# Modulation vectors summed over the partitions: plain fp32 sums as the moving operand, one row each, in place of split halves as the stationary operand

## The chip, the cores and the metric

The kernel runs on one core of one Trainium2 chip. The metric is the time of one execution on the device, in microseconds (us); the median of several runs counts.

## What is computed

The reference is a two-part transformer: two layers with Fourier, neighbourhood and latent attention branches and a feed-forward part, on 512 latent and 256 context tokens of width 1024, and then a second block with a mixture of experts. Every normalization is followed by a modulation, whose shift, scale and gate vectors come from a conditioning vector. Only this matters here:

```python
silu_c = jax.nn.silu(c)
silu_cc = jax.nn.silu(c_ctx)
for l in range(DEPTH):
    ...
    sh1, sc1, g1, sh2, sc2, g2 = [m[:, None, :] for m in jnp.split(silu_c @ w_mod[l] + b_mod[l], 6, axis=-1)]
    csh1, csc1, cg1, csh2, csc2, cg2 = jnp.split(silu_cc @ w_mod[l] + b_mod[l], 6, axis=-1)
    a_lat = x_lat * (1 + sc1) + sh1
```

Each `w_mod` is 1024 x 6144 in fp32; the second block has its own, with one conditioning vector.

## The kernel before

Activations lie transposed in SBUF: features on the 128 partitions, tokens along the row. A dense layer (`run_dense`) goes through *pieces*: a piece is one output tile of 128 features. For each piece SP loads 128 columns of weights (`w_raw`, two buffers in turn), ACT copies them to fp32r (`w_hi`, L1118), DVE subtracts that from the original (`w_lo`, L1128), and TensorE (PE) multiplies: `w_hi` and `w_lo` with the high half of the activations (L1101, L1102), `w_hi` with their low half (L1104). Thus three fp32r products stand for one fp32 product. Results lie in PSUM banks 0 to 3 for even pieces and 4 to 7 for odd ones; ACT or DVE takes them out. SP waits for `w_lo` of the piece two before (`lo_ready`) and then loads the next weights.

The modulation vectors of what comes later are made beside such a dense layer, by `Vectors` (L815), a *background* of `run_dense`. It takes `w_mod` in chunks of 512 columns. A chunk is four loads of 256 x 512 values (`vec_w`, two buffers, L857). For each of the `nv` conditioning vectors DVE multiplies the weights by the vector's value of each partition and adds up over the eight row tiles (`vec_acc`, L877 and L880). What is left is a sum over the partitions, for which TensorE serves: `vec_acc` is split into an fp32r half on ACT (`vec_hi`, L902) and the rest on DVE (`vec_lo`, L865), and these are the *stationary* operands, 128x128 at a time, against two columns of ones (`ones_r`). So the vector comes out with features on the partitions, 128 of them a matmul, in bank 3:

```python
pe.wait_ge(*self.sem(vec_lo, k + 1))
for q in range(4):
    for v in range(self.nv):
        o = 3 * BANK + ((4 * k + q) * self.nv + v) * 2
        for part in (self.hi, self.lo):
            m = pe.matmul(ps[:, o:o + 2], part[:, v, q * P:(q + 1) * P], ones_r[:], start=(part is self.hi), stop=(part is self.lo))
```

After the last chunk DVE adds the bias (L889) and 1 to the scales (L894).

The order on each engine is written out by hand, by the number of the piece. At piece n an engine first does its part of the splitting for piece n+1, then `behind(n)`, the background's share, and then takes out the results of piece n; TensorE does `behind(n)` ahead of its matmuls of piece n. If the last sums of a chunk fall at piece n, its halves are made at n+1 (ACT behind the cast of the weights, DVE behind `w_lo`), and its matmuls stand ahead of piece n+2. `vec_used` counts the steps of sums that DVE has done; SP waits for it before it loads the next `vec_w`, and what SP issues behind that, the weights of the next piece included, comes later. What is left when the pieces have run out is done by `rest` at the stage's end.

`Vectors` runs three times: in the first projection of layer 0 (20 pieces, 8 chunks, two vectors, a chunk every 2 pieces from piece 4 on, thus the last chunk's matmuls are in `rest`), in the feed-forward stage of layer 0 (60 pieces, 12 chunks, two vectors, a chunk every 4 pieces from piece 2 on) and in that of layer 1 (60 pieces, 12 chunks, one vector). During the first of these POOL makes bias tables for the neighbourhood attention: it gathers small pieces from DRAM (L1753, eight DMAs a table, three tables) and adds masks (L1756).

## Time and profile before

| | |
|---|---|
| median of 3 runs | 3252.98 us (3251.86 to 3255.18) |
| the profiled execution's own time | 3246.34 us |
| its span in the profile | 3244.5 us |
| PE busy | 2950.4 us (91%) |
| DVE busy | 1679.8 us (52%) |
| ACT busy | 1228.2 us (38%) |
| POOL busy | 411.5 us (13%) |
| mean granted clock of TensorE | 0.956 |
| PE, small matmuls of the vectors (L912) | 208 of `vec_hi`, 208 of `vec_lo` |
| DVE, sums (L880) | 364 of 128x512, 257.7 us |

The profile comes from one execution, whose instructions are recorded; its time is not that of the other runs. The span is what the records cover. PEld is the loading of stationary operands, which runs beside matmuls. The ends of matmuls are modelled, so the time that a matmul takes from the ones behind it is read from the distance of the starts. The clock of TensorE is given as a share of full speed (1.00 is 2.4 GHz, 0.50 is 1.2 GHz). Register, branch, semaphore and DMA-issuing instructions don't count as busy.

### The profile page before, as it was taken

What the parts mean: (1) busy time and instruction counts of PE and PEld (TensorE: products, weight loads), DVE (VectorE), ACT (ScalarE), POOL (GpSimd) and SP (SyncE); (2) the same over time, 40 slices, a digit from 0 to 9 for tenths busy, and PEclk for the clock granted to TensorE, in tenths of its full rate; (3) what the DMA queues carried; (4) which work ended last, traced back from release to release, by engine and by line L of the source; (5) the groups of instructions that cost most, each with busy time, mean ns of one, the idle gap of its engine ahead of it and who ended that gap; (6) DMA issues with size and microseconds to landing.
All of it is one profiled execution on the core that took longest, in us unless ns stands there. A gap on an engine that the chain in (4) does not pass through costs nothing. (4 is left out here: it accounts for less than half of the span.)

```text
span 3244.5 us, 37650 instructions
## 1 busy us (share of the span) xinstructions
PE 2950.4 (91%) x15073; PEld 2353.4 (73%) x15073; DVE 1679.8 (52%) x2334; ACT 1228.2 (38%) x1821; POOL 411.5 (13%) x395
## 2 busy tenths in 40 slices
PE   7898889999979999999798799998999968876995
PEld 4787556888868888887587457886888736554784
DVE  3575665223345555543416554446655354645896
ACT  5324545122243211221535443225322144535884
POOL 4400400000010000002402100000000004202332
PEclk9899999999989999999899899999999988897997
DMA  7861101222114443332610104324656236334962
GB/s 205 147 176 37 24 1 39 63 65 60 55 39 130 120 121 104 117 90 49 95 53 16 24 10 107 98 72 143 186 160 181 72 47 72 150 109 144 374 238 78
DMA packets 397873, 330.15 MB, mean 102 GB/s; under 512 B 38038, under 2 KB 340484, under 8 KB 397572
## 3 DMA queue, kind: packets, MB, share of 16 engines
q1 hardware_dynamic: 384196, 304.56, 33.3%
q0 software_dynamic: 13248, 23.13, 3.5%
q8 instruction: 120, 1.97, 0.3%
q14 instruction: 53, 0.43, 0.1%
q10 hardware_dynamic: 256, 0.07, 0.0%
HBM read 331.96 MB, written 30.33 MB: 112 GB/s over the span
## 5 line engine op out<-in xcount | busy, mean ns | idle before, releaser
L1101 PE MATMUL ps<-ahi,w_hi 128*128 128x512 f32 (+1 forms) x2264 | 770.8, 354 | 6.6 <-DVE w_lo L1128 6.6
L1102 PE MATMUL ps<-ahi,w_lo 128*128 128x512 f32 (+1 forms) x2264 | 768.0, 353 | 0.0
L1128 DVE TENSOR_TENSOR w_lo<-w_raw,w_hi 128x1024 fp32r<-128x1024 f32 (+2 forms) x244 | 352.0, 1444 | 389.9 <-ACT w_hi L1118 388.1
L1101 PEld LDWEIGHTS ps<-ahi,w_hi 128*128 128x128 f32 x2264 | 428.1, 189 | 69.3 <-DVE w_lo L1128 9.8
L1104 PE MATMUL ps<-alo,w_hi 128*128 128x512 f32 (+1 forms) x2264 | 474.1, 352 | 0.0
L1102 PEld LDWEIGHTS ps<-ahi,w_lo 128*128 128x128 f32 x2264 | 428.4, 189 | 59.6
L1118 ACT CAST w_hi<-w_raw 128x1024 fp32r<-128x1024 f32 (+2 forms) x244 | 285.3, 1171 | 488.7 <-PE ps L1104 378.8
L1104 PEld LDWEIGHTS ps<-alo,w_hi 128*128 128x128 f32 x2264 | 376.8, 189 | 58.8
L880 DVE SCALAR_TENSOR_TENSOR vec_acc<-vec_w,csilu,vec_acc 128x512 f32<-128x512 f32 x364 | 257.7, 753 | 10.8 <-DMA vec_w<-in_w_mod 5.7
L1204 POOL TENSOR_TENSOR xsum<-x 128x768 f32<-128x768 f32 (+1 forms) x4 | 7.2, 1801 | 1421.8 <-DVE x L1189 1421.8
L1189 DVE SCALAR_TENSOR_TENSOR x<-ps,mod,x 128x512 f32<-128x512 f32 x80 | 51.4, 668 | 250.6 <-PE ps L1104 235.2
L1101 PE MATMUL ps<-hhi,w_hi 128*128 128x512 f32 (+1 forms) x462 | 157.8, 356 | 0.0
L1102 PE MATMUL ps<-hhi,w_lo 128*128 128x512 f32 (+1 forms) x462 | 157.5, 355 | 0.0
L1224 ACT CAST hhi<-hf 128x768 fp32r<-128x768 f32 (+1 forms) x44 | 32.0, 728 | 282.1 <-DVE hf L1232 282.1
L3105 ACT CAST e_hi<-e_raw 128x2048 fp32r<-128x2048 f32 x69 | 131.6, 1913 | 14.9 <-DMA e_raw<-in_w_up 9.6
L1670 POOL TENSOR_SCALAR prob<-prob,nm 128x512 f32<-128x512 f32 (+3 forms) x64 | 79.5, 1242 | 394.5 <-DVE nm L1595 394.5
L1306 DVE TENSOR_TENSOR gp<-sg,ps 128x768 f32<-128x768 f32 (+1 forms) x32 | 26.3, 821 | 196.7 <-PE ps L1104 179.6
L1297 ACT ACTIVATE sg<-ps 128x768 f32<-128x768 f32 (+1 forms) x48 | 33.8, 705 | 241.0 <-PE ps L1104 241.0
L1164 ACT COPY proj<-ps 128x512 f32<-128x512 f32 (+2 forms) x58 | 39.6, 748 | 191.9 <-PE ps L1104 180.0
L1971 PE MATMUL ps<-mla_pt,proj 128*128 128x512 f32 x192 | 102.5, 616 | 0.0
L1102 PEld LDWEIGHTS ps<-hhi,w_lo 128*128 128x128 f32 x462 | 86.9, 188 | 13.0
L1101 PEld LDWEIGHTS ps<-hhi,w_hi 128*128 128x128 f32 x462 | 86.9, 188 | 13.0
(525 smaller groups left out, 5299.4 us busy)
## 6 DMA issues: line engine op xcount, KB each, us to landing
vec_w<-in_w_mod SPq DMA_DIRECT2D x128, 512.0 KB, 3.9
w_raw<-in_w_in SPq DMA_DIRECT2D x102, 512.0 KB, 4.3
e_raw<-in_w_gate SPq DMA_DIRECT2D x46, 512.0 KB
e_raw<-in_w_up SPq DMA_DIRECT2D x46, 512.0 KB
e_raw<-in_w_down SPq DMA_DIRECT2D x46, 512.0 KB
w_raw<-in_w_ffn_gate SPq DMA_DIRECT2D x44, 512.0 KB, 3.9
w_raw<-in_w_ffn_up SPq DMA_DIRECT2D x44, 512.0 KB, 3.9
w_raw<-in_w_ffn_down SPq DMA_DIRECT2D x32, 704.0 KB, 4.7
```

Of the source, the lines that this page charges most:

```text
L880: m = dve.scalar_tensor_tensor(out=acc, in0=w, scalar=f, in1=acc, op0=ALU.mult, op1=ALU.add)
L1101: pe.matmul(o, whi[:, j, b0 + b, :], hi[:, b, t0:t0 + tn], start=(b == 0), stop=False)
L1102: pe.matmul(o, wlo[:, j, b0 + b, :], hi[:, b, t0:t0 + tn], start=False, stop=False)
L1104: m = pe.matmul(o, whi[:, j, b0 + b, :], lo[:, b, t0:t0 + tn], start=False, stop=(b == nb - 1))
L1118: act.copy(whi[:, j, 0:d.blocks, :], raw_of(d, i, jj)).then_inc(hi_ready[j].sem, 1)
L1128: dve.tensor_tensor(wlo[:, j, 0:d.blocks, :], raw_of(d, i, jj), whi[:, j, 0:d.blocks, :].bitcast(F32), ALU.subtract).then_inc(lo_ready[j]. ...
L1164: m = act.copy(o_, s_) if scale is None else act.activation(o_, s_, ACT.Identity, scale=scale)
L1189: m = dve.scalar_tensor_tensor(out=xo, in0=ps[:, b + t0:b + t0 + tn], scalar=mod[:, v, bass.ds(i * 2 + (gate + jj), 1)], in1=xo, op0=ALU.m ...
L1297: act.activation(sg[:, jj, :], ps[:, 4 * BANK * jj:4 * BANK * jj + T], ACT.Sigmoid).then_inc(gated.sem, 1)
L1670: pool.tensor_scalar(self.prob[:, j, slot, 0:u.keys], self.prob[:, j, slot, 0:u.keys], self.nm[:, j, slot, 3:4], None, ALU.mult).then_inc( ...
L1971: m = pe.matmul(ps[:, bank:bank + LAT], weight(b, j), self.pt[:, s % 3, :], start=(b == 0), stop=(b == kt - 1))
L3105: act.copy(whi[:, n % HI, :], raw[:, n % RAW, :]).then_inc(e_hi.sem, 1)
```

## The change

The sums are no longer split. They become the *moving* operand of a plain fp32 matmul, 512 columns at once, one matmul a vector. The stationary operand is a window of `pick_row`, a table of 128 x 47 zeros with one column of ones in the middle: the window of `rows` columns (`rows` = chunks x vectors: 16, 24 and 12) that has the ones at place r puts the sum over the partitions into row r of the output and adds zeros to all other rows. All chunks accumulate in one region of bank 3 (`start` only for row 0, `stop` only for the last row), which ends as a matrix of `rows` x 512. DVE copies that to SBUF (into a buffer of sums that is free by then), TensorE transposes it in four parts of 128 columns, and DVE adds the bias as before, with another pattern of addresses. `vec_acc` has two buffers, so that DVE goes on with the next chunk at once. ACT has no part any more. TensorE waits for `vec_used`, that is for the sums themselves, at the same piece as before; the copy comes one piece after the last matmuls, the transposes another piece later, and the bias at the end, two pieces later than before.

```diff
@@ -56,6 +56,7 @@
+VEC_ROWS = 24
...
-        vec_used, vec_hi, vec_lo, vec_mm, vec_chain = (tally(n) for n in ("vec_used", "vec_hi", "vec_lo", "vec_mm", "vec_chain"))
+        vec_used, vec_mm, vec_chain = (tally(n) for n in ("vec_used", "vec_mm", "vec_chain"))
...
-        ones_r = sb(root, "ones_r", [P, 2], F32R)
+        pick_row = sb(root, "pick_row", [P, 2 * VEC_ROWS - 1])
...
                     ch.link(dve.memset(ones[:], 1.0))
-                    ch.mark(dve.tensor_copy(ones_r[:], ones[:, 0:2]))
+                    ch.link(dve.tensor_scalar(pick_row[:], ones[:, 0:2 * VEC_ROWS - 1], 0.0, None, ALU.mult))
+                    ch.mark(dve.tensor_copy(pick_row[:, VEC_ROWS - 1:VEC_ROWS], ones[:, 0:1]))
...
                 self.raw = sb(c, "vec_w", [P, 2, self.STEP, self.CN])
-                self.acc = sb(c, "vec_acc", [P, self.nv, self.CN])
-                self.hi = sb(c, "vec_hi", [P, self.nv, self.CN], F32R)
-                self.lo = sb(c, "vec_lo", [P, self.nv, self.CN], F32R)
+                self.acc = sb(c, "vec_acc", [P, 2, self.nv, self.CN])
+                self.rows = self.chunks * self.nv
+                self.row = self.acc[0:self.rows, self.chunks % 2, 0, :]
                 self.norm_first = norm_first
                 self.when = [start + n // self.per_chunk * pieces + n % self.per_chunk * pieces // self.per_chunk for n in range(self.steps)]
                 last = [self.when[(k + 1) * self.per_chunk - 1] for k in range(self.chunks)]
                 self.at = {}
                 for s_, n in enumerate(self.when):
                     self.at.setdefault(n, []).append(s_)
-                self.hi_at = {n + 1: k for k, n in enumerate(last)}
-                self.lo_at = {n + 1: k for k, n in enumerate(last)}
                 self.mm_at = {n + 2: k for k, n in enumerate(last)}
-                assert len(self.hi_at) == self.chunks
-                self.end = last[-1] + 4
-                self.c0 = {t: t.base for t in (*vec_loaded, vec_used, vec_hi, vec_lo, vec_mm, vec_chain)}
+                assert len(self.mm_at) == self.chunks
+                self.copied_at, self.turned_at = last[-1] + 3, last[-1] + 4
+                self.end = last[-1] + 6
+                self.c0 = {t: t.base for t in (*vec_loaded, vec_used, vec_mm, vec_chain)}
...
             def run(self, who, eng, n):
-                {"sp": self.sp, "dve": self.dve, "act": self.act, "pe": self.pe}[who](eng, n)
+                if who != "act":
+                    {"sp": self.sp, "dve": self.dve, "pe": self.pe}[who](eng, n)
...
@@ -857,20 +859,14 @@
                     sp.dma_start(self.raw[:, s_ % 2], self.wv[:, self.STEP * kp:self.STEP * (kp + 1), c0:c0 + self.CN]).then_inc(vec_loaded[s_ % 2].sem, 16)
 
             def dve(self, dve, n):
-                if n in self.lo_at:
-                    k = self.lo_at[n]
-                    dve.wait_ge(*self.sem(vec_hi, k + 1))
-                    if k >= 1:
-                        dve.wait_ge(*self.sem(vec_mm, k))
-                    dve.tensor_tensor(self.lo[:], self.acc[:], self.hi[:].bitcast(F32), ALU.subtract).then_inc(vec_lo.sem, 1)
                 for s_ in self.at.get(n, []):
                     k, kp = s_ // self.per_chunk, s_ % self.per_chunk
                     dve.wait_ge(*self.sem(vec_loaded[s_ % 2], 16 * (s_ // 2 + 1)))
-                    if kp == 0 and k >= 1:
-                        dve.wait_ge(*self.sem(vec_lo, k))
+                    if kp == 0 and k >= 2:
+                        dve.wait_ge(*self.sem(vec_mm, k - 1))
                     for q in range(self.STEP):
                         for v, a in enumerate(self.cols):
-                            acc, w = self.acc[:, v, :], self.raw[:, s_ % 2, q, :]
+                            acc, w = self.acc[:, k % 2, v, :], self.raw[:, s_ % 2, q, :]
                             f = csilu[:, a, self.STEP * kp + q:self.STEP * kp + q + 1]
                             done = (s_ * self.STEP + q) * self.nv + v
                             if kp == 0 and q == 0:
@@ -881,44 +877,45 @@
                             m.then_inc(vec_chain.sem, 1)
                     dve.wait_ge(*self.sem(vec_chain, (s_ + 1) * self.STEP * self.nv))
                     dve.sem_inc(vec_used.sem, 1)
+                if n == self.copied_at:
+                    dve.wait_ge(*self.sem(vec_mm, self.chunks))
+                    dve.tensor_copy(self.row, ps[0:self.rows, 3 * BANK:4 * BANK]).then_inc(vec_chain.sem, 1)
                 if n == self.end - 1:
-                    dve.wait_ge(*self.sem(vec_mm, self.chunks))
+                    dve.wait_ge(*self.sem(vec_mm, self.chunks + 1))
                     t0, nt = self.first // P, self.chunks * 4
                     for v in range(self.nv):
-                        src = ps[:, 3 * BANK:3 * BANK + nt * 2 * self.nv].rearrange("p (t v two) -> p t v two", v=self.nv, two=2)[:, :, v, 0]
-                        m = dve.tensor_tensor(self.dst[:, v, t0:t0 + nt], src, self.bias[:, t0:t0 + nt], ALU.add)
+                        src = ps[:, 3 * BANK:3 * BANK + 4 * self.rows].rearrange("p (q k v) -> p k q v", q=4, v=self.nv)[:, :, :, v]
+                        m = dve.tensor_tensor(self.dst[:, v, t0:t0 + nt].rearrange("p (k q) -> p k q", q=4), src,
+                                              self.bias[:, t0:t0 + nt].rearrange("p (k q) -> p k q", q=4), ALU.add)
                     m.then_inc(vec_chain.sem, 1)
-                    dve.wait_ge(*self.sem(vec_chain, self.steps * self.STEP * self.nv + 1))
+                    dve.wait_ge(*self.sem(vec_chain, self.steps * self.STEP * self.nv + 2))
                     for s_ in (1, 2, 4, 5) if self.nv == 2 else (1, 4):
                         if s_ * KT >= t0:
                             dve.tensor_scalar(self.dst[:, 0:self.nv, s_ * KT:(s_ + 1) * KT], self.dst[:, 0:self.nv, s_ * KT:(s_ + 1) * KT], 1.0, None, ALU.add)
 
-            def act(self, act, n):
-                if n in self.hi_at:
-                    k = self.hi_at[n]
-                    act.wait_ge(*self.sem(vec_used, (k + 1) * self.per_chunk))
-                    if k >= 1:
-                        act.wait_ge(*self.sem(vec_mm, k))
-                    act.copy(self.hi[:], self.acc[:]).then_inc(vec_hi.sem, 1)
-
             def pe(self, pe, n):
                 if n in self.mm_at:
                     k = self.mm_at[n]
-                    pe.wait_ge(*self.sem(vec_lo, k + 1))
+                    pe.wait_ge(*self.sem(vec_used, (k + 1) * self.per_chunk))
+                    for v in range(self.nv):
+                        r = k * self.nv + v
+                        own = pick_row[:, VEC_ROWS - 1 - r:VEC_ROWS - 1 - r + self.rows]
+                        m = pe.matmul(ps[0:self.rows, 3 * BANK:4 * BANK], own, self.acc[:, k % 2, v, :], start=(r == 0),
+                                      stop=(r == self.rows - 1), skip_group_check=True)
+                    m.then_inc(vec_mm.sem, 1)
+                if n == self.turned_at:
+                    pe.wait_ge(*self.sem(vec_chain, self.steps * self.STEP * self.nv + 1))
                     for q in range(4):
-                        for v in range(self.nv):
-                            o = 3 * BANK + ((4 * k + q) * self.nv + v) * 2
-                            for part in (self.hi, self.lo):
-                                m = pe.matmul(ps[:, o:o + 2], part[:, v, q * P:(q + 1) * P], ones_r[:], start=(part is self.hi), stop=(part is self.lo))
+                        o = 3 * BANK + q * self.rows
+                        m = pe.transpose(ps[:, o:o + self.rows], self.row[:, q * P:(q + 1) * P], ident[0:self.rows, 0:self.rows])
                     m.then_inc(vec_mm.sem, 1)
 
             def ended(self):
                 for b in range(2):
                     vec_loaded[b].base += 16 * len([s_ for s_ in range(self.steps) if s_ % 2 == b])
                 vec_used.base += self.steps
-                for t in (vec_hi, vec_lo, vec_mm):
-                    t.base += self.chunks
-                vec_chain.base += self.steps * self.STEP * self.nv + 1
+                vec_mm.base += self.chunks + 1
+                vec_chain.base += self.steps * self.STEP * self.nv + 2
```

How the instructions stand afterwards, at the places of interest. First DVE in the first projection, where the first chunk is complete and the second begins; a row is line, operation, output and inputs by name, shape, and in brackets the semaphores that it waits for. Before:

```order
L880 SCALAR_TENSOR_TENSOR vec_acc<-vec_w,csilu,vec_acc 128x512 [waits vec_chain] x3
L1128 TENSOR_TENSOR w_lo<-w_raw,w_hi 128x1024 [waits vec_chain,hi_ready1]
L865 TENSOR_TENSOR vec_lo<-vec_acc,vec_hi 128x1024 [waits vec_hi]
L877 TENSOR_SCALAR vec_acc<-vec_w,csilu 128x512 [waits vec_lo,vec_loaded0]
L877 TENSOR_SCALAR vec_acc<-vec_w,csilu 128x512
L880 SCALAR_TENSOR_TENSOR vec_acc<-vec_w,csilu,vec_acc 128x512 [waits vec_chain] x2
```

With the change the same place on DVE reads so:

```order
L876 SCALAR_TENSOR_TENSOR vec_acc<-vec_w,csilu,vec_acc 128x512 [waits vec_chain] x3
L1125 TENSOR_TENSOR w_lo<-w_raw,w_hi 128x1024 [waits vec_chain,hi_ready1]
L873 TENSOR_SCALAR vec_acc<-vec_w,csilu 128x512 [waits vec_loaded0]
L873 TENSOR_SCALAR vec_acc<-vec_w,csilu 128x512
L876 SCALAR_TENSOR_TENSOR vec_acc<-vec_w,csilu,vec_acc 128x512 [waits vec_chain] x2
```

The subtraction is gone, and the next chunk's sums wait for their load alone.

Second, DVE at the end of the same stage (`vec_5` is the bias, `mod_8` the vectors), from the last sums to the branch out of the block. Before:

```order
L880 SCALAR_TENSOR_TENSOR vec_acc<-vec_w,csilu,vec_acc 128x512 [waits vec_chain,vec_loaded1]
L880 SCALAR_TENSOR_TENSOR vec_acc<-vec_w,csilu,vec_acc 128x512 [waits vec_chain] x3
L865 TENSOR_TENSOR vec_lo<-vec_acc,vec_hi 128x1024 [waits vec_chain,vec_mm,vec_hi]
L889 TENSOR_TENSOR mod_8<-ps,vec_5 128x32 [waits vec_mm]
L889 TENSOR_TENSOR mod_8<-ps,vec_5 128x32
L894 TENSOR_SCALAR mod_8<-mod_8 128x2x8 [waits vec_chain]
```

With the change, again DVE at the end of the stage:

```order
L876 SCALAR_TENSOR_TENSOR vec_acc<-vec_w,csilu,vec_acc 128x512 [waits vec_chain,vec_loaded1]
L876 SCALAR_TENSOR_TENSOR vec_acc<-vec_w,csilu,vec_acc 128x512 [waits vec_chain] x3
L882 COPY vec_acc<-ps 16x512 [waits vec_chain,vec_mm]
L888 TENSOR_TENSOR mod_8<-ps,vec_5 128x32 [waits vec_mm]
L888 TENSOR_TENSOR mod_8<-ps,vec_5 128x32
L894 TENSOR_SCALAR mod_8<-mod_8 128x2x8 [waits vec_chain]
```

The subtraction has made room for a copy of 16 rows, which waits for TensorE.

Third, TensorE at that end: the last dense matmuls of the stage, what the vectors add, and the next stage's first. With the change:

```order
L1101 MATMUL ps<-alo,w_hi 128x256 x8
L903 MATMUL ps<-vec_acc,pick_row 16x512 [waits vec_used]
L903 MATMUL ps<-vec_acc,pick_row 16x512
L910 MATMUL ps<-ident,vec_acc 128x16 [waits vec_chain]
L910 MATMUL ps<-ident,vec_acc 128x16 x3
L1009 UNCONDITIONAL_BRANCH
```

Where L903 stands there were sixteen matmuls L912, in turn of `vec_hi` and `vec_lo`, the first of which waited for `vec_lo`; L910 is new.

## Rows read from the trace of the kernel before

**Rows 1.** The page: busy us (share of the span) x instructions of TensorE.

```profile
PE 2950.4 (91%) x15073; PEld 2353.4 (73%) x15073; DVE 1679.8 (52%) x2334; ACT 1228.2 (38%) x1821; POOL 411.5 (13%) x395
```

**Rows 2.** Stretches: us, busy us (count) by engine, clock, DMA share, GB/s.

```profile
0.00:60.00 60.00, 43.85 (x211) 22.31 (x211) 19.19 (x50) 24.52 (x46) 28.78 (x60) 1.00 0.70 216
60.00:160.00 100.00, 87.58 (x468) 75.85 (x469) 48.59 (x56) 44.13 (x64) 43.95 (x50) 0.90 0.87 151
1100.00:1300.00 200.00, 200.00 (x1183) 177.13 (x1182) 104.12 (x133) 37.00 (x38) 0.00 (x0) 1.00 0.38 114
```

**Rows 3.** Tiles of sums' halves: count, ns min/median/max, first and last start.

```profile
L912 PE MATMUL ps<-ones_r,vec_hi x208: 165/250/371, 127.3 to 2524.0; 128*128 128x2 f32 x104
L865 DVE TENSOR_TENSOR vec_lo<-vec_acc,vec_hi x32: 682/1217/1767, 122.5 to 2521.6; 128x1024 fp32r<-128x1024 f32 x20, 128x512 fp32r<-128x512 f32 x12
```

**Rows 4.** Timeline, PE, end of a group: start us, us, line, tiles, count.

```profile
127.26 0.17 PE L912 MATMUL ps<-ones_r,vec_hi 128*128 128x2 f32 x1
128.96 0.47 PE L1101 MATMUL ps<-ahi,w_hi 128*128 128x512 f32 x1
129.28 0.39 PE L1102 MATMUL ps<-ahi,w_lo 128*128 128x512 f32 x1
129.51 0.40 PE L1101 MATMUL ps<-ahi,w_hi 128*128 128x512 f32 x1
```

**Rows 5.** Timeline, PE: plain fp32 matmuls (each is two records).

```profile
53.17 3.62 PE L311 MATMUL ps<-proj,mod_c 128*2 128x256 f32 x16
928.76 10.59 PE L606 MATMUL ps<-vec_w,ones 128*128 128x512 f32 x32 [1.93 <-ACT vec_w L622]
```

**Rows 6.** Timeline, DVE, 122 to 164 us; in brackets the idle time before.

```profile
122.50 1.77 DVE L865 TENSOR_TENSOR vec_lo<-vec_acc,vec_hi 128x1024 fp32r<-128x1024 f32 x1
124.37 1.66 DVE L877 TENSOR_SCALAR vec_acc<-vec_w,csilu 128x512 f32<-128x512 f32 x2
140.00 2.74 DVE L880 SCALAR_TENSOR_TENSOR vec_acc<-vec_w,csilu,vec_acc 128x512 f32<-128x512 f32 x4 [4.07 <-DMA vec_w<-in_w_mod]
152.07 1.32 DVE L1128 TENSOR_TENSOR w_lo<-w_raw,w_hi 128x1024 fp32r<-128x1024 f32 x1 [9.32 <-ACT w_hi L1118]
162.17 1.23 DVE L1128 TENSOR_TENSOR w_lo<-w_raw,w_hi 128x1024 fp32r<-128x1024 f32 x1
```

**Rows 7.** SP and POOL issues, landing of the 132.41 issue, ACT's cast behind it.

```profile
132.41 0.64 SPq L1040 DMA_DIRECT2D w_raw<-in_w_in  x1
DMA to landing us min/median/max: 18.6/18.6/18.6
130.37 6.04 POOL L1753 DMA_DIRECT2D proj<-rpb_rows  x8 [0.32 <-POOL na_bias L1756]
150.99 1.04 ACT L1118 CAST w_hi<-w_raw 128x1024 fp32r<-128x1024 f32 x1 [12.51 <-DMA w_raw<-in_w_in]
```

**Rows 8.** PE around the stall: timeline, and two stretches with the clock.

```profile
155.11 0.37 PE L912 MATMUL ps<-ones_r,vec_hi 128*128 128x2 f32 x1 [9.21 <-DVE vec_lo L865]
158.54 0.77 PE L1101 MATMUL ps<-ahi,w_hi 128*128 128x512 f32 x1
149.00:150.00 1.00, 0.00 (x0) 0.84 1.14 262
163.00:164.00 1.00, 1.00 (x5) 0.84 0.82 104
```

**Rows 9.** Timeline, PE and DVE, end of the first stage.

```profile
260.68 1.12 PE L1104 MATMUL ps<-alo,w_hi 128*128 128x256 f32 x8
264.90 0.27 PE L912 MATMUL ps<-ones_r,vec_hi 128*128 128x2 f32 x1 [3.09 <-DVE vec_lo L865]
267.78 0.29 DVE L889 TENSOR_TENSOR mod<-ps,vec 128x32 f32<-128x32 f32 x2 [2.94 <-PE ps L912]
```

**Rows 10.** Timeline, PE: transposes of the prologue; tile view, DVE copies from PSUM.

```profile
25.34 1.09 PE L302 MATMUL ps<-ident,proj 128*128 128x128 f32 x8
L1606 DVE COPY proj<-ps x18: 404/682/692, 331.3 to 2838.0; 128x512 f32<-128x512 f32 x14, 128x256 f32<-128x256 f32 x4
```

## Prediction

> **What bounds the kernel now.** I read the busy times first, then a table of stretches, then the tiles that the change touches, then the timelines of single engines around them. TensorE is busy 2950.4 of 3244.5 us [rows 1]. Background sums for the modulation vectors run beside three dense stages: the first projection (60 to 268 us, 8 chunks of two vectors), the feed-forward of layer 0 (960 to 1530 us, 12 chunks of two vectors) and that of layer 1 (2220 to 2590 us, 12 chunks of one vector). In the feed-forward stages TensorE is busy 200.00 of 200.00 us at clock 1.00, while DVE has 104.12 and ACT 37.00 us [rows 2]: there only TensorE's own work counts, and DVE's and ACT's vector work is hidden. The first projection is different: from 60 to 160 us the clock is 0.90 and TensorE is busy 87.58 of 100 us [rows 2], so it stands still somewhere.
>
> **What is removed.** ACT's cast of each chunk's sums and DVE's subtraction (32 of each; the subtraction 1217 ns at the median) go [rows 3]. Hidden in the feed-forward stages, they are worth nothing there: the cover is the dense matmuls, and without it the two would cost some 2.5 us a chunk. TensorE loses 416 small matmuls, 208 for each half [rows 3].
>
> **TensorE, per chunk.** With two vectors a chunk is 16 small matmuls. The first starts at 127.26, the dense ones go on at 128.96; the first dense interval behind them is 0.32 us where the next is 0.23 us [rows 4]. So a group costs 1.70 + 0.09 = 1.79 us, 0.112 us each, and 0.90 us with one vector. The new group is one plain fp32 matmul of 512 columns per vector. Its price: 16 records of 512 and 16 of 256 columns in 10.59 us, thus 24 units of 512 columns; less a tail of some 0.2 us that is 0.43 us a record, two records a matmul [rows 5]. That gives 0.86 us a vector, 1.72 us for two. That its stationary operand has 12 to 24 columns, not 128, should not matter: records with 2 stationary columns and 256 moving ones take 3.62 us for 16, 0.22 us each, the same rate [rows 5]. The gain is 0.07 us a chunk with two vectors and 0.04 us with one: 18 chunks x 0.07 + 12 x 0.04 = 1.8 us (two of the first stage's chunks are counted below). Added are four transposes a stage. Eight of 128x128 take 1.09 us, 0.12 us each without the tail [rows 10], so 0.5 us in each feed-forward stage, 1.0 us together. Net: **0.8 us gained**. Bounds: nothing to 2 us.
>
> The Trainium skill (FP8 and Floating Point Precision, TensorE Precision Notes) counts four passes for true fp32. Four dense passes of 0.23 us [rows 4] would be 0.92 us a matmul, against the 0.86 us of the row; the sum would then lose 52 x 0.06 = 3 us. I go by the row, which is the very kind of matmul.
>
> The copy out of PSUM (DVE, 682 ns at the median for 128x512 [rows 10]) and the transposes' wait for it cost nothing in the feed-forward stages: DVE runs the copy right behind the splitting for the next piece, TensorE asks for it one piece later, and a piece is 8 us or more. Behind the waiting transposes stands that next piece; it would be late only if the copy were 5 us late. The tables' block of zeros costs two tiny DVE instructions at the start, where DVE waits for loads: nothing. The loads themselves are unchanged in number and order on SP's queue; POOL's is not passed.
>
> **The stall at 146 us.** TensorE waits 9.21 us, until 155.11, for DVE's low half of a chunk's sums [rows 8]. But DVE's low half stood behind its splitting of weights, which started at 152.07 and ended at 153.39 [rows 6], and that behind ACT's cast at 150.99, which had waited 12.51 us for a transfer of weights [rows 7]. This transfer was issued at 132.41 on SP's queue, among eight gathers that POOL issues from 130.37 on, and took 18.6 us [rows 7]. Then TensorE worked through the small group first, at half clock, and real work began at 158.54; the clock was at its lower level from about 149.7 to 163.3 (0.84 is the mean of a microsecond with 0.32 of it at half clock) [rows 8].
>
> Now the sums of that chunk are complete before 146 us (DVE's last adds end at 142.74 [rows 6]), TensorE waits for them alone, and the 1.7 us of new matmuls fall into the stall. It then restarts when the weights are split: 153.4 in place of 155.11, 1.7 us earlier, and without 3.43 us of small matmuls at half clock, which are 1.7 us at full clock. If nothing else moved, that is **3.4 us**.
>
> Something else moves. DVE's subtraction at 122.50 takes 1.77 us before the next chunk's sums start at 124.37 [rows 6]. SP's loads of that chunk wait for these sums, and the weight transfer is issued behind them on the same queue. So I take the issue at 132.41 to come 1.9 us earlier, at 130.5, when one gather is out and not three. I take the landing to move by the same 1.9 us. Total for the stall: **5.3 us**. Lower bound 3.4 (the landing stays, since the gathers stay). Upper bound: TensorE's standstill shrinks to 4 us or less, and the clock may never fall; it fell 3.7 us after TensorE stopped. The 8.2 us at half clock from 155.1 on would then lose nothing, 4 us more: 9.3 us.
>
> The Trainium skill (DMA: Bandwidth & Descriptors, Queues, rings and completion order) says that a DMA engine serves the queues with work in turn, packet by packet. By that the weights still share with the gathers that come later, so the landing would move by no more than the issue does; if the queues were served in order of issue it would move by several us. The single 18.6 us does not tell the two apart.
>
> **The end of the first stage.** The last chunk comes after the last dense piece. TensorE stops at 261.80, ACT casts, DVE subtracts, the small group runs from 264.90 (partly at half clock) and DVE's add starts at 267.78 [rows 9]: 5.98 us. Now: 4 records x 0.43 = 1.72, the drain of the last 0.17, copy 0.68, four transposes 0.36 with 0.27 of tail, two hand-overs of 0.05: 3.3 us. The add and what follows are the same. **2.7 us gained**; bounds 1.5 (some of it at half clock) to 3.
>
> **Sum.** 0.8 + 5.3 + 2.7 = 8.8 us. The profiled execution took 3246.34 us with a span of 3244.5; it would be 3237.5. It lies 6.6 us below the median of the runs, 3252.98, so the unprofiled runs may stall a little longer. I carry the difference over: 3252.98 - 8.8 = **3244.2 us**. About 0.2% (6.5 us) is what a measurement of this kernel can tell from no change.
>
> **Rivals.**
> 1. *The clock stays up in the stall.* If the weights land at 148 us or before, TensorE resumes before the clock falls. Gain 9.3 in place of 5.3, sum 12.8, time 3240.2. For it: the standstill is only about 2 us longer than the time in which the clock fell. Against it: the landing must move by more than the issue.
> 2. *The stall is given back one piece later.* DVE has two steps of sums between one splitting (ended 153.39) and the next (162.17 to 163.40) [rows 6]: 8.3 us without the subtraction, about as long as a piece of TensorE at full clock. These sums need loads that stand in the same crowded queue. If the landings don't move and these sums are late by 3 us or so, the stall yields 0 to 1 us, and the total is 0.8 + 0.5 + 2.7 = 4 us: 3249 us, no measurable change. For it: DVE is in order, and three loads queue behind the gathers.
> 3. *Slower: the new matmuls run at half clock.* The feed-forward stages have no slack on TensorE. If matmuls that use 12 to 24 columns of the array let the clock fall, each of the 52 costs 0.86 us more; all of them are 45 us, 3289 us. It decides from 18 matmuls on (8.8 + 6.5 us over 0.86). Against it: the prologue, with 2 stationary columns in most matmuls, holds 1.00 from 0 to 60 us [rows 2], and the small groups of today don't bring it down either [rows 2].
>
> **How the numbers follow.** Forecast as worked out 0.45 (its own range 3241 to 3246.5), rival 1 0.20, rival 2 0.28, rival 3 0.07. The first two are faster by over 0.2%: 0.65. Same 0.28, slower 0.07. The range takes in rival 1 and most of rival 2: 3237 to 3251.
>
> **What would show it.** In the new profile: two fp32 matmuls a chunk as four records 0.43 us apart, at clock 1.00 in the feed-forward stages; TensorE's wait near 146 us ended by a weight splitting and not by sums, at 151.5; dense work there 5 us or more ahead of before; the last dense matmul of the first stage to DVE's add in 3.3 us; both feed-forward stages within 1 us of before. I am wrong if the weight transfer lands no earlier, if a new wait follows within 20 us, or if records of the new matmuls are longer than 0.43 us apart.

## The result and the profile after

The changed kernel takes **3230.6 us** (median of 6 runs, 3227.54 to 3235.27); the kernel before, in runs beside them, 3251.0 us (3241.18 to 3255.18). The ratio is 0.9941, 95% interval 0.9925 to 0.9957. The same two kernels, compared again on two later occasions, gave 0.9960 (0.9946 to 0.9973) and 0.9945 (0.9929 to 0.9960): 13 to 18 us. The prediction was 3244.2 us, range 3237 to 3251: right in its sign, but the gain is about twice the 8.8 us of its sum, and the time lies below the range.

The profiled execution took 3230.32 us with a span of 3228.5 us. The stretches that answer to [rows 2] and [rows 8] (microseconds; then each engine's busy time, TensorE's granted clock, DMA share, GB/s):

```profile
60.00:160.00 100.00, 94.77 (x494) 78.95 (x495) 56.16 (x64) 43.76 (x64) 46.06 (x50) 0.95 0.75 169
149.00:150.00 1.00, 1.00 (x3) 0.10 (x1) 1.00 (x3) 0.79 (x2) 0.00 (x0) 1.00 0.84 295
1100.00:1300.00 200.00, 200.00 (x1125) 169.01 (x1124) 98.62 (x128) 31.93 (x34) 0.00 (x0) 1.00 0.38 113
```

From 60 to 160 us TensorE is busy 94.77 us, 7.2 more than in [rows 2], and the clock is 0.95 there. What is left of half clock lies between 60 and 90 us, where both kernels have some (0.83, 0.90 and 0.76 in the three tens of microseconds before, 0.83, 0.92 and 0.74 after): the prediction read the 0.90 of [rows 2] as the stall's alone. In the feed-forward stage it is busy throughout, as before, at clock 1.00: rival 3 (new matmuls at half clock) is out. The timeline of TensorE between 136 and 151 us, against [rows 8]:

```profile
136.99 1.12 PE L1101 MATMUL ps<-alo,w_hi 128*128 128x256 f32 x8
139.79 0.50 PE L1098 MATMUL ps<-ahi,w_hi 128*128 128x512 f32 x1 [1.68 <-DVE w_lo L1125]
...
148.37 1.89 PE L903 MATMUL ps<-vec_acc,pick_row 128*16 128x512 f32 x4
150.19 0.50 PE L1098 MATMUL ps<-ahi,w_hi 128*128 128x512 f32 x1
```

The wait of 9.21 us is gone, and with it the half clock behind it: rival 1's picture, but by more than rival 1 had it, since the only wait left there is 1.68 us at 139.79. It belongs to another piece: the transfer that is crowded now was issued at 122.27 and took 12.8 us to land. The transfers that the prediction reasoned about have moved far. This is POOL's timeline, for [rows 7]:

```profile
92.42 5.30 POOL L1750 DMA_DIRECT2D proj<-rpb_rows  x7 [0.30 <-POOL na_bias L1753]
104.77 0.77 POOL L1750 DMA_DIRECT2D proj<-rpb_rows  x1 [7.04 <-issue]
117.93 6.05 POOL L1750 DMA_DIRECT2D proj<-rpb_rows  x8 [0.32 <-POOL na_bias L1753]
```

POOL's third table of gathers goes at 117.93 us, not at 130.37 [rows 7]. In the kernel before, the eighth gather of the second table waited longer as well:

```profile
94.63 5.31 POOL L1753 DMA_DIRECT2D proj<-rpb_rows  x7 [0.30 <-POOL na_bias L1756]
113.10 0.76 POOL L1753 DMA_DIRECT2D proj<-rpb_rows  x1 [13.16 <-issue]
```

At 113 us nothing that the prediction speaks of has happened yet: the first subtraction whose absence could free DVE is the one at 122.50 [rows 6]. So something in the change acts earlier and elsewhere. This was the question of the experiments.

The end of the first stage, for [rows 9], is TensorE's timeline and then DVE's:

```profile
251.15 1.12 PE L1101 MATMUL ps<-alo,w_hi 128*128 128x256 f32 x8
252.19 1.89 PE L903 MATMUL ps<-vec_acc,pick_row 128*16 128x512 f32 x4
254.86 0.41 PE L910 MATMUL ps<-ident,vec_acc 16*128 16x16 f32 x4 [0.77 <-DVE vec_acc L882]
```

```profile
254.12 0.68 DVE L882 COPY vec_acc<-ps 16x512 f32<-16x512 f32 x1 [6.02 <-PE ps L903]
255.31 0.29 DVE L888 TENSOR_TENSOR mod<-ps,vec 128x32 f32<-128x32 f32 x2 [0.51 <-PE ps L910]
```

From the end of the dense matmuls (252.27) to DVE's add (255.31) are 3.04 us, where they were 5.98 and the prediction said 3.3.

### The profile page after: what moved, and what is told of

Same layout as the page of the kernel before. It is cut to its first block and busy times, and to the rows that moved or that the text cites. A ratio compares the mean times of both kernels' runs of the same rounds, so it can differ in the third digit from the quotient of the medians.

```text
span 3228.5 us, 36929 instructions
## 1 busy us (share of the span) xinstructions
PE 2949.7 (91%) x14773; PEld 2309.6 (72%) x14773; DVE 1651.2 (51%) x2306; ACT 1203.4 (37%) x1789; POOL 417.6 (13%) x395
## 3 DMA queue, kind: packets, MB, share of 16 engines
q0 software_dynamic: 13248, 23.13, 3.0%
## 5 line engine op out<-in xcount | busy, mean ns | idle before, releaser
L876 DVE SCALAR_TENSOR_TENSOR vec_acc<-vec_w,csilu,vec_acc 128x512 f32<-128x512 f32 x364 | 261.5, 764 | 13.6 <-DMA vec_w<-in_w_mod 9.1
L1294 ACT ACTIVATE sg<-ps 128x768 f32<-128x768 f32 (+1 forms) x48 | 33.8, 705 | 241.0 <-PE ps L1101 241.0
L1218 ACT ACTIVATE sg<-ps 128x768 f32<-128x768 f32 (+1 forms) x44 | 31.0, 704 | 179.1 <-PE ps L1101 178.8
```

Source lines behind the costliest of these rows:

```text
L876: m = dve.scalar_tensor_tensor(out=acc, in0=w, scalar=f, in1=acc, op0=ALU.mult, op1=ALU.add)
L1294: act.activation(sg[:, jj, :], ps[:, 4 * BANK * jj:4 * BANK * jj + T], ACT.Sigmoid).then_inc(gated.sem, 1)
```

## The experiments

There were sixteen runs: thirteen kernels with one edit or two, and three repetitions of the kernels before and after. Times are medians; every ratio is to the kernel before in runs on the same chip, comes from all runs of both, and can differ from the quotient of the medians by up to 0.0011. Two lengths recur: that of the **first stage**, from TensorE's first `ahi,w_hi` matmul to its first `latent_sq,ones` matmul behind 230 us, read from each profile (208.4 us before, 195.7 after), and the start of POOL's third table.

### Undo one part of the change: the wait, or DVE's work

`before_again` is the kernel before, `after_again` the changed one.

> The kernel before, unchanged, for a second profile. The profile of before stalled TensorE for 9.2 us at 146 us (13 us with the half clock), that of the change for 1.7 us. Theory A (the change removes the stall): the stall is here again, 9 us or more, and the time is 3245 to 3255 us. Theory B (the gathers' timing is luck and the two profiles differ by it): the stall is here of another size, under 5 us, or absent, and the time differs from the 3251.0 us of before by 5 us or more.

> The change, unchanged, for a second profile and as the base of the two variants. Theory A: a stall of 0 to 3 us near 140 us, time 3227 to 3235 us. Theory B: a stall of 5 us or more also happens with the change.

`after_oldwait` puts the wait back: TensorE's group also waits for a one-column DVE copy at the place of the old subtraction (the edit, shortened).

```diff
+self.late_at = {n + 1: k for k, n in enumerate(last)}
+self.late = sb(c, "vec_late", [P, 1])
 # dve
+if n in self.late_at: dve.tensor_copy(self.late[:], ones[:, 0:1]).then_inc(vec_late.sem, 1)
 # pe
+pe.wait_ge(*self.sem(vec_late, k + 1))
```

> The change, but TensorE's matmuls of a chunk also wait for a mark (a copy of one column on DVE) that stands where DVE's subtraction stood, behind the splitting of the next weights. DVE's time stays free. If the place of the wait makes the gain, the matmuls fall behind the stall again: 3.5 us or more slower than the change (3234 or more). If DVE's earlier sums and the earlier transfers behind them make it: within 2 us of the change.

`after_dvetime` puts DVE's work back (a subtraction of 128 x nv x 512 at the old place), and TensorE does not wait for it.

> The change, plus a subtraction of the old size on DVE at the old place, whose result nobody reads; TensorE doesn't wait for it. If the sums that start 1.8 us earlier, and with them the loads, make the gain at the stall: most of it goes, 8 to 12 us slower than the change (3239 to 3243), with a stall over 6 us at 140 to 155 us in the profile. If the place of the wait makes it: within 2 us of the change.

Measured: before_again 3249.63 us, 1.0003 (0.9990 to 1.0017). after_again 3232.23, 0.9960. The stall is there again in before_again (9.0 us), and after_again has a wait of 3.6 us: the two profiles did not differ by luck. after_dvetime 3231.90, 0.9948 (0.9934 to 0.9962): DVE's work costs nothing that can be measured. after_oldwait 3252.19, 1.0019 (1.0006 to 1.0033): all the gain gone, which looks like proof that the wait was worth 20 us. The profile says no. The first stage of after_oldwait is 198.6 us, as short as in after_again (199.0), and POOL's third table goes at 116.3 us. Its time is lost in the feed-forward stages, where all dense matmuls are the same: the part that the kernel before runs from 924 to 1529 us takes 614.6 us where the changed kernel takes 604.5, and the one from 2191 to 2593 us takes 408.3 in place of 401.9: together 16.5 of the 20 us. One period of the feed-forward in each (stretches, granted clock 1.00 in both):

```profile
1306.90:1341.80 34.90, 34.90 (x197) 29.31 (x196) 18.78 (x24) 7.07 (x8) 0.00 (x0) 1.00 0.41 120
```

```profile
1279.20:1314.90 35.70, 35.70 (x198) 29.68 (x197) 18.84 (x25) 7.06 (x8) 0.00 (x0) 1.00 0.39 119
```

The first is the changed kernel, the second after_oldwait: the same matmuls, never idle, 0.8 us longer. What did differ was where they read from. In the built programs, pick_row (47 columns, 192 bytes) takes the room of ones_r (2 columns, 32 bytes), so the tiles behind it lie 160 bytes further on in their partitions: proj, na_bias, ahi, alo, vec_w and the first stage's w_raw start at 96 modulo 256 bytes before, and at 0 after. And the mark tile of after_oldwait, 4 bytes that take up 32, pushes the feed-forward's w_raw, w_hi and w_lo from 192 to 224 modulo 256 (they are at 32 in the kernel before).

### Move the tiles, change no instruction

`before_moved` is the kernel before with one tile widened, `after_unmoved` the changed kernel with all tiles back at their old places modulo 256, `oldwait_moved` is after_oldwait with a mark tile of 64 bytes, which puts the feed-forward's three tiles at 0 modulo 256, `after_all64` aligns x, the mods and the latent attention's tiles too (warm allocated ahead of mods, three pads).

```diff
-ones_r = sb(root, "ones_r", [P, 2], F32R)
+ones_r = sb(root, "ones_r", [P, 2 * 24 - 1], F32R)[:, 0:2]                 # before_moved
-pick_row = sb(root, "pick_row", [P, 2 * VEC_ROWS - 1])
+pick_row = sb(root, "pick_row", [P, 72])[:, 0:2 * VEC_ROWS - 1]            # after_unmoved
-self.late = sb(c, "vec_late", [P, 1])
+self.late = sb(c, "vec_late", [P, 16])                                     # oldwait_moved
```

> Kernel before, with one edit: the tile ones_r is 47 columns wide in place of 2 (only its first 2 are used). No instruction changes; every SBUF tile behind it lies 160 bytes further on in its partition, which is where the change puts them (in the built programs ahi, alo, proj, na_bias and the first stage's w_raw, w_hi, w_lo begin at 96 modulo 512 bytes before and at 256 after: from 32 to 0 modulo 64). Theory A (places: the 20 us of the change come from where the tiles lie, by faster DMA landings in the first stage and closer matmuls later): ratio to before 0.994 to 0.996, about 3235 us, POOL's third table of gathers from about 117 us, the stall at 154 us gone or under 4 us. Theory B (waits: they come from the vectors' chain, which is as before here): ratio 0.999 to 1.001, the stall of 9 us stays. The DVE matmul group and the tail of the first stage stay as before under both, worth 2.7 us.

> Changed kernel with pick_row allocated 72 columns wide (47 used), so that all tiles behind it lie 96 bytes further on: 32 modulo 64, as before the change. No instruction changes. Theory A (places): most of the gain goes, ratio 0.998 to 1.001; what stays is the shorter tail, some 3 us (0.999). The third table of gathers goes from about 130 us again and a stall of some 9 us may come back. Theory B (waits): as the changed kernel, 0.994 to 0.996.

> after_oldwait with its mark tile 16 columns wide in place of 1 (64 bytes, not 32), so that the tiles behind it keep the places of the changed kernel: in after_oldwait the FF stages' w_raw, w_hi, w_lo lay at 32 modulo 64. PE still waits for a DVE mark at the place of the old vec_lo. Theory A (places): the 20 us that after_oldwait lost come back, ratio 0.994 to 0.997, and a period of the FF chunks of 34.9 us in place of 35.67. Theory B (the wait costs the time): ratio 1.001 to 1.003 again.

> Changed kernel with the remaining large tiles that lie at 32 modulo 64 bytes (x, both mod tiles, the latent attention's eye, wv, spread, k32, pt and rs, fox_ck) moved to 0 modulo 64: warm is allocated ahead of mods, and three small pads. No instruction changes. Theory A (any large tile at 32 modulo 64 costs): 1 to 6 us faster than the changed kernel, ratio about 0.993; Theory A' (only the tiles that DMA writes and TensorE reads count, nearly all of which lie right already): as the changed kernel, 0.994 to 0.996. Theory B: the same 0.994 to 0.996.

Measured: **before_moved 3236.09 us, 0.9959 (0.9946 to 0.9971)**: the old code, moved by 160 bytes, has most of the change's gain. after_unmoved 3236.96, 0.9966 (0.9950 to 0.9982): the new code at the old places has most of it too. oldwait_moved 3235.78, 0.9956 (0.9942 to 0.9969): with the same instructions nearly all that after_oldwait lost is back, so it was the places and not the wait. But the period of 34.9 us that was expected of it did not come: it is 35.4 us, and the two feed-forward parts take 611.4 and 398.8 us. after_all64 3230.33, 0.9941: as the changed kernel; moving the other tiles has no effect that can be measured.

So theory A holds for before_moved and oldwait_moved and fails for after_unmoved, whose 0.9966 is closer to B. POOL's timeline shows that its gathers are late again all the same. First before_moved, then after_unmoved:

```profile
104.73 0.80 POOL L1753 DMA_DIRECT2D proj<-rpb_rows  x1 [7.67 <-issue]
...
117.37 6.04 POOL L1753 DMA_DIRECT2D proj<-rpb_rows  x8 [0.32 <-POOL na_bias L1756]
```

```profile
111.07 0.76 POOL L1750 DMA_DIRECT2D proj<-rpb_rows  x1 [11.23 <-issue]
...
127.81 6.05 POOL L1750 DMA_DIRECT2D proj<-rpb_rows  x8 [0.32 <-POOL na_bias L1753]
```

The gathers themselves land sooner. Layer 1 has the same 24 gathers with no vectors beside them, and their times from issue to landing are, first in the kernel before, then in before_moved:

```profile
DMA to landing us min/median/max: 4.1/9.1/13.7
```

```profile
DMA to landing us min/median/max: 4.0/7.2/9.4
```

The page's queue part shows it for the whole program. These are the lines of POOL's queue (packets, MB, share of 16 engines' span), again before and before_moved: the same packets in less time. Not all of them are gathers: the kernels that leave out 16 of the 48 have 768 packets and 2.1 MB fewer.

```profile
q0 software_dynamic: 13248, 23.13, 3.5%
```

```profile
q0 software_dynamic: 13248, 23.13, 3.1%
```

SP's queue gains too (33.3% before, 32.7% in before_moved): the three loads of 1 MB into na_bias before the first stage land in 8.5 us in place of 10.5. Its loads of vec_w beside the vectors do not, once the gathers are done: 3.7 us in both from 175 to 245 us, with 5.1 and 4.9 us for w_raw.

There are then two cures for one stall. after_unmoved has the crowded transfers, and what is left of the stall is a wait of 3.67 us and 3.4 us at half clock (152.9 to 156.3), in place of 9.21 and 13.6. Here the prediction can be read line by line, because the tiles lie as before. SP's timeline with the landing of that issue, and TensorE's:

```profile
130.52 0.47 SPq L1037 DMA_DIRECT2D w_raw<-in_w_in  x1
DMA to landing us min/median/max: 18.4/18.4/18.4
```

```profile
146.28 1.89 PE L903 MATMUL ps<-vec_acc,pick_row 128*16 128x512 f32 x4 [0.32 <-DVEq L879]
151.84 0.50 PE L1098 MATMUL ps<-ahi,w_hi 128*128 128x512 f32 x1 [3.67 <-DVE w_lo L1125]
```

Predicted: issue at 130.5, landing moved by as much, new matmuls inside the stall, dense work from 151.5 us. It is 130.52, 148.9 (where it was 151.0) and 151.84. One thing is otherwise: the chunk's last sums, which the prediction has done by 142.74, end at 146.17, because their load comes later, and TensorE waits 0.32 us for them.

### Which alignment, and is it the gathers?

`before_moved96` and `before_moved256` widen ones_r to 32 and 72 columns. `before_fewgathers` and `after_fewgathers` leave out the second and third table's gathers in layer 0 (`for r in range(ROWS if l or not b else 0)`).

> Kernel before with ones_r 32 columns wide: every tile behind it lies 96 bytes further on, at 192 modulo 256 bytes (0 modulo 64, 64 modulo 128) where before it was 96 modulo 256. No instruction changes. Theory A64 (what counts is a start at 0 modulo 64 bytes): as before_moved, ratio 0.995 to 0.997, third table of gathers from about 117 us and landed 16 us after its first issue. Theory A256 (what counts is that the 128-byte pieces of the gathers don't cross a multiple of 256 bytes, as they don't in before_moved and the changed kernel; the DMA: Bandwidth & Descriptors page of the Trainium skill, section How a descriptor splits into AXI transactions, has such a rule for where a descriptor starts): as the kernel before, 0.999 to 1.001, third table from 130 us and landed 19 to 20 us after its first issue. Theory B (waits, not places): as before, 1.000.

> Kernel before with ones_r 72 columns wide: every tile behind it lies 256 bytes further on, the same modulo 256 as before. Theories A64 and A256: as the kernel before, ratio 0.999 to 1.001, third table of gathers from 130 us. If any shift helps (luck of the placement, nothing about alignment), it may be 0.995 to 0.998.

> Kernel before, without the gathers of the second and third table of layer 0's bias (16 of 24; the additions read the first table's landing again, so layer 0's bias is not the reference's). Theory A (the stall at 154 us comes of these gathers, which hold w_raw's landing up): no stall and no half clock, 8 to 13 us faster in the first stage, ratio 0.995 to 0.997. Theory B (the stall comes of the chain of DVE and the vectors, not of the gathers): the stall of 9 us at vec_lo stays, ratio 0.999 to 1.001.

> Changed kernel without the same 16 gathers. What is left of the change when there is no stall to cure. Theory A: against before_fewgathers 3 to 5 us (the tail's 3 and little more), against the changed kernel 0 to 3 us; so a ratio of 0.993 to 0.995 to before. Theory B: as the changed kernel against before, and 16 us against before_fewgathers.

Measured, with the first stage's length, the third table's start and the median time to landing of layer 1's gathers (us; the last row is new code, the others are old):

```
                  starts at (mod 256)  third table  layer 1's gathers  first stage  ratio
before                    96             130.4             9.1            208.4     1
before_moved256           96             129.8             8.6            208.7     1.0001 (0.9987 to 1.0015)
before_moved96           192             125.3             8.3            205.3     0.9991 (0.9977 to 1.0005)
before_moved               0             117.4             7.2            200.8     0.9959 (0.9946 to 0.9971)
before_fewgathers         96              -                9.2            194.9     0.9966 (0.9951 to 0.9981)
after_fewgathers           0              -                7.2            193.8     0.9954 (0.9940 to 0.9967)
```

A shift by itself does nothing (256 bytes: 1.0001). A start at 0 modulo 64 bytes is not enough either (192: 0.9991, no difference that can be measured), so A64 falls. Of the three starts tried, only 0 modulo 256 gives the gain. A gather writes 64 pieces of 128 bytes next to each other in each partition. The Trainium skill (DMA: Bandwidth & Descriptors, How a descriptor splits into AXI transactions) says that a transaction starts at a multiple of 256 bytes, that what lies between it and the descriptor's start costs beats of 32 bytes all the same, and that a piece over such a multiple needs a second transaction. An estimate worked out from it: an average piece costs 6 beats at 0, 8 at 192 and 9 at 96. Against before_moved, layer 1's gathers take 1.1 us more at 192 and 1.9 at 96 (1.4 in before_moved256), and the third table's delay is 7.9 and 13.0 us: the order is the rule's, and the sizes are not far from its 2 to 3. That is agreement and no proof. The page words the rule for reads, while what moved here is the destination, and no run shows how a piece is split.

Without the gathers the stall of 9.21 us doesn't exist, and the old code gains 11 to 13 us: the gathers make it. after_fewgathers differs from before_fewgathers by some 3 us (3232.57 against 3236.04, intervals that overlap): where there is no stall to cure, little more than the tail is left of the change, and of the places too, since these two kernels lie at 0 and 96 and their first stages differ by 1.1 us. So it is through the gathers that the places count here.

### With the tiles at their old places: the wait, or DVE's work, again

`unmoved_oldwait` is after_unmoved with the old place of the wait (its mark tile takes 256 bytes, so that the others stay modulo 256), `unmoved_dvetime` is after_unmoved with DVE's old work, for which TensorE does not wait. `after_start2` starts the first stage's vectors two pieces earlier, and `after_again2` is the changed kernel.

> after_unmoved (the changed code with every large tile where it was before, modulo 256 bytes) plus the old place of the wait: PE's group also waits for a one-column DVE copy that stands where the subtraction into vec_lo stood. DVE's time stays free. If the place of the wait is what carries the change at the old places (theory W): the stall of 9 us and the half clock come back, ratio 0.9985 to 1.000 (the shorter tail stays), some 7 us over after_unmoved. If the work taken off DVE carries it (theory D): as after_unmoved, 0.996 to 0.9975. If neither (theory P, the places alone and luck): anything from 0.997 to 1.001 with the gathers as late as before.

> after_unmoved plus DVE's old work: a subtraction of the size of the old one at its old place, which PE does not wait for. Theory W (place of the wait): as after_unmoved, 0.996 to 0.9975. Theory D (DVE's work, my prediction's 1.9 us and what the clock makes of it): 0.998 to 0.9995, PE's first stall after 140 us 2 us or more longer than in after_unmoved (3.7).

> Changed kernel with the first stage's vectors started two pieces earlier (start=2 in place of 4), so that the copy, the turn and the additions into mod fall into pieces that still have other matmuls. Estimate from the changed kernel's tail (3.04 us between the last group and the additions, of which some 2 us would be covered): 1 to 3 us faster than the changed kernel, ratio 0.993 to 0.995. Rival: the vec_w loads, two pieces earlier, fall among the gathers of the second table and hold w_raw up, so PE stalls earlier: 0.996 to 1.000.

> The changed kernel itself, to stand beside after_start2 and the two unmoved kernels on the same chip: ratio 0.994 to 0.996.

Measured: **unmoved_oldwait 3243.06, 0.9985 (0.9975 to 0.9994)**; unmoved_dvetime 3239.44, 0.9970 (0.9957 to 0.9983), as after_unmoved (0.9966). The medians favour theory W: the place of the wait carries the gain, and DVE's freed work can't be seen. They lie only 3.6 and 6.1 us apart, and the intervals overlap a little, so the timeline is the firmer evidence. TensorE in unmoved_oldwait, and then the stretch behind:

```profile
151.45 3.57 PE L910 MATMUL ps<-vec_acc,pick_row 128*16 128x512 f32 x4 [7.33 <-DVE vec_late L867]
154.95 0.80 PE L1106 MATMUL ps<-ahi,w_hi 128*128 128x512 f32 x1
```

```profile
152.00:155.00 3.00, 3.00 (x5) 0.34 (x3) 3.00 (x4) 1.94 (x2) 3.00 (x4) 0.50 0.01 4
```

The group runs behind the stall and at half clock (0.50; 3.57 us where it is 1.89), and dense work begins at 154.95, 3.1 us later than in after_unmoved. In unmoved_dvetime the weights' issue is back at 132.7 and TensorE goes on at 152.42:

```profile
152.42 0.50 PE L1106 MATMUL ps<-ahi,w_hi 128*128 128x512 f32 x1 [2.69 <-DVE w_lo L1133]
```

That is 0.6 us later than in after_unmoved, for an issue 2.2 us later: the weights land at 149.6 in place of 148.9. The sums' earlier start is worth 0.6 us in these two profiles, not 1.9.

after_start2 (`start=2` for `start=4` in the first stage) 3233.99 us, 0.9960 (0.9945 to 0.9975), against 3230.05, 0.9945, for after_again2: no gain, as the rival in its expectation had it. It covers the tail, but the loads of vec_w now come among the gathers of the second table, and a wait of 5.9 us for w_lo stands where after_again2 has 4.8. No kernel tried is faster than the changed one by more than the intervals.

## Why the prediction was wrong

**The step that failed is a term that the sum priced at nothing.** "The tables' block of zeros costs two tiny DVE instructions at the start ... nothing" is true of the instructions. But the table is 188 bytes where ones_r was 8, and every tile behind it moves. That alone is worth 12 to 13 us to the old code (0.9959), more than the whole forecast, and it carries the changed kernel from after_unmoved's 3237.0 us to some 3231 (after_all64, beside it, 3230.3). "The loads themselves are unchanged in number and order" was right, and so was the silence on POOL; what changed is how long the same packets take.

**The stall: mechanism right, the total near at the old places.** after_unmoved is the kernel that the prediction described. Its ratio 0.9966 is 11 us (5.8 to 16.3), the forecast's 8.8 us (0.9973) is inside. Its first stage is 9.1 us shorter than before (199.3 against 208.4); predicted 5.3 + 2.7 = 8.0. Dense work goes on 6.6 us earlier, counted from the stage's start, and the tail gives 2.9; from there to the last dense matmul 0.5 us is lost. Of the two parts of the 5.3, the place of the wait (3.4) measured 3.1 in TensorE's timeline and 3.6 to 6 us in the medians (3243.06 against unmoved_dvetime's 3239.44 and after_unmoved's 3236.96), and DVE's earlier sums (1.9) measured 0.6, with nothing to be seen in the medians. What failed there is "I take the landing to move by the same 1.9 us". In this pair of profiles it did (18.4 us to landing against 18.6 [rows 7]), but over all six at the old places it doesn't: issues at 132.4 to 132.7 land at 149.6 to 151.0 and issues at 129.9 and 130.5 at 148.7 and 148.9. How the queues share is not decided by it. What the 5.3 did not count is the clock: the sum left the 8.2 us at half clock behind the stall as they were, and after_unmoved has 3.4.

**The clock.** Rival 1 had the right outcome, but nothing in it says why. It asked that the weights land by 148 us, against its own doubt that the landing must move by more than the issue; they do land early (135.1 us for those of the wait at 139.79), because the gathers are done early. In the first profile of the changed kernel the clock stays at 1.00 through the wait of 1.68 us; in after_again and after_again2 the wait is 3.56 and 4.8 us and the stretch 140 to 150 has 0.83. So even the changed kernel sometimes pays a few us there. Rivals 2 and 3 did not happen: no new wait follows in after_unmoved within 20 us.

**TensorE's group.** The records of the new matmuls are 0.43 us apart, as forecast, but the seams between them and the dense ones were not in the sum. From the last dense matmul's start (1306.71) to the next dense one (1308.74) are 2.03 us, with 0.21 us into the group and 0.52 out of it; before it is 1.82 (1320.81 to 1322.63). So a group loses 0.2 us where 0.07 was to be gained, 3.6 us over the 18 chunks with two vectors if the dense matmuls kept their pace. They don't: a whole period (from group to group) takes 34.9 or 35.3 us in the changed kernel and 35.1 before, with the 256-column matmuls 0.113, 0.118 and 0.118 us apart. The two cancel, and the feed-forward stages stay the same (604.6 us before, 604.5 after; 401.6 and 401.9). "Within 1 us of before" was right, by luck.

**The tail** was right: 2.9 us measured, 2.7 predicted.

**Not additive.** The places give 12 to 13 us, the code 11 at the old places, both together 13 to 20. Each cures the same stall, and the second to come has only the tail and what is left of the wait. Had the prediction known of the places, its sum would have been some 13 + 3 us (an estimate), 3237 us from its base, and 3235 from the 3251.0 us of the runs beside the changed kernel: still 4 us above it.

**Still open.** Why the pace of the same matmuls takes a few fixed values (periods of 34.9, 35.1, 35.3, 35.4 and 35.7 us). Both profiles of the kernel before have 35.1, and all three of the changed kernel 34.9 with some 35.3. The tiles' places have to do with it (35.7 in after_oldwait, 35.4 in oldwait_moved, the same code), and the added wait by itself does not slow it (34.9 and 35.3 in unmoved_oldwait, which has it too); but before and before_moved, which lie differently, both have 35.1. And the 5 us or so between the changed kernel and after_unmoved are located only in part. Their first stages are as long as each other (195.7 to 200.1 and 199.3), and the two intervals overlap a little. From the end of layer 0's feed-forward part to the latent attention of layer 1, a stretch with layer 1's gathers (1528.6 to 1710.4 us in the kernel before), the changed kernel takes 180.0 to 180.8 us in its three profiles and after_unmoved 184.0, with 3.4 us of waiting for w_lo; but unmoved_dvetime takes 181.2 and before_moved 184.7 there, so one profile each does not settle it.

## What to carry to other kernels

A tile's size is part of a change: widening or narrowing one small tile near the bottom of SBUF moves the tiles behind it, and transfers in small pieces can slow down or speed up far from the edit, as the gathers did here. Compare the starts of the tiles before and after, and when an experiment adds a tile, keep the others where they were; otherwise it measures the places, as after_oldwait did. And where two parts of a change can cure one stall, try each alone on the kernel before: the loss from taking one out shows little.

## What was not expected of the hardware

The same gathers land in 9.1 us at the median with destinations at 96 modulo 256 bytes and in 7.2 at 0 (layer 1), and POOL's queue takes 3.5% and 3.1% of the engines' span for the same 13248 packets; the third table of the first stage starts 13 us earlier. A destination at 0 modulo 64 but 192 modulo 256 lies between (8.3 us). And dense fp32r matmuls, never idle and at a granted clock of 1.00, can be 2% slower over a whole stage (614.6 us against 604.5, a period of 35.7 against 34.9) in a kernel with one wait and one small copy a chunk and a 4-byte tile more. Of these it is not the wait or the copy: unmoved_oldwait has them too, its tiles lie otherwise, and its stage takes 605.2 us.
